# One table set for logarithm and exponential, reworked layer norms, and the last norm made in halves

## What is computed

```python
def _layer_norm(x, g, b):
    mu = jnp.mean(xf, axis=-1, keepdims=True)
    var = jnp.mean(jnp.square(xf - mu), axis=-1, keepdims=True)
    y = (xf - mu) * lax.rsqrt(var + LN_EPS)
    return (y * g + b)

def rmsnorm(x, g):
    y = x32 * lax.rsqrt(jnp.mean(x32 * x32, axis=-1, keepdims=True) + EPS)
    return (y * g)

# first block, per layer (0: attention, 1: retention)
h = _layer_norm(DEEPNORM_ALPHA * h + mix, ln_g[layer, 0], ln_b[layer, 0])
h = _layer_norm(DEEPNORM_ALPHA * h + _sq_relu_mlp(h, ffn_w1[layer], ffn_w2[layer]), ln_g[layer, 1], ln_b[layer, 1])
# second block
h = rmsnorm(x, norm_mix[layer])          # attention and state-space scan from h, added to x
h = rmsnorm(x, norm_ffn[layer])
x = x + (jax.nn.silu(gate) * val) @ w_ffn_down[layer]
return rmsnorm(x, norm_final)
```

## Time and profile before

| | us |
|---|---|
| median of 3 runs | 2658.95 (2658.17 to 2660.28) |
| span of the profiled execution, first to last instruction | 2656.4 |
| TensorE matmuls busy in it | 2615.0 |
| VectorE busy | 1675.5 |
| ScalarE busy | 1268.0 |

### The profile page before, as it was taken

How to read it: one execution, slowest core, us unless ns; L and a number is a source line. 1 busy time by engine, 2 the same in 40 slices (tenths; PEclk the granted TensorE clock), 3 DMA queues, 4 the chain that set the end, 5 groups by cost and what they waited for, 6 DMA issues and landing times.

```text
span 2656.4 us, 42476 instructions
## 1 busy us (share of the span) xinstructions
PE 2615.0 (98%) x16497; PEld 2236.1 (84%) x16497; DVE 1675.5 (63%) x2902; ACT 1268.0 (48%) x2049; POOL 183.4 (7%) x234
## 2 busy tenths in 40 slices
PE   9999999999999999999999999999999999999998
PEld 9877799999999798779898786766877777799996
DVE  4544586264565465487265535875589987696784
ACT  4556365153454354365154434254365564475561
POOL 1111000000000000100000012051000000000000
PEclk9999999999999999999999999999999999999999
DMA  9994936858556564736557979922433333254451
GB/s 355 222 230 119 216 92 234 207 165 248 135 171 212 146 184 140 232 110 196 145 164 245 260 187 266 253 66 80 145 94 114 119 111 120 81 189 148 156 174 56
DMA packets 187722, 450.56 MB, mean 170 GB/s; under 512 B 14984, under 2 KB 31368, under 8 KB 186896
## 3 DMA queue, kind: packets, MB, share of 16 engines
q1 hardware_dynamic: 108368, 264.29, 29.4%
q0 software_dynamic: 60000, 167.78, 26.7%
q10 hardware_dynamic: 19168, 15.93, 2.0%
HBM read 438.24 MB, written 159.51 MB: 225 GB/s over the span
## 4 chain that ended last, share of the span: by engine, by line
PE 85%; DVE 8%; ACT 4%; issue 2%; DMA 0%; POOL 0%; DVEq 0%; ACTq 0%; POOLq 0%
PE ps L399 29%; PE ps L1546 25%; PE ps L549 6%; PE ps L3344 4%; PE ps L2354 2%; PE ps L1991 2%; PE ps L2145 2%; PE ps L2029 2%; PE ps L2891 2%; PE ps L791 2%; PE ps L919 2%; DVE w_lo L370 1%; PE ps L878 1%; ACT w_hi L362 1%; DVE xs L3044 1%
## 5 line engine op out<-in xcount | busy, mean ns | idle before, releaser
L370 DVE TENSOR_TENSOR w_lo<-raw,w_hi 128x1024 fp32r<-128x1024 f32 x500 | 611.1, 1223 | 467.1 <-ACT w_hi L362 466.1
L362 ACT ACTIVATE w_hi<-raw 128x1024 fp32r<-128x1024 f32 x500 | 527.1, 1055 | 512.9 <-PE ps L399 292.3
L1546 PE MATMUL ps<-x_hi,w_hi 128*128 128x264 f32 (+1 forms) x1120 | 317.4, 283 | 2.1 <-DVE rg L1925 0.7
L1546 PE MATMUL ps<-x_hi,w_lo 128*128 128x264 f32 (+1 forms) x1120 | 316.3, 282 | 0.0
L1546 PE MATMUL ps<-x_lo,w_hi 128*128 128x264 f32 (+1 forms) x1120 | 316.1, 282 | 0.0
L399 PE MATMUL ps<-x_hi,w_hi 128*128 128x512 f32 (+1 forms) x688 | 248.3, 378 | 4.4 <-DVE x_lo L1410 2.7
L399 PE MATMUL ps<-x_lo,w_hi 128*128 128x512 f32 (+1 forms) x688 | 244.3, 372 | 0.0
L399 PE MATMUL ps<-x_hi,w_lo 128*128 128x512 f32 (+1 forms) x688 | 243.2, 371 | 0.0
L1546 PEld LDWEIGHTS ps<-x_hi,w_hi 128*128 128x128 f32 x1120 | 210.8, 188 | 5.0 <-issue 2.2
L1546 PEld LDWEIGHTS ps<-x_hi,w_lo 128*128 128x128 f32 x1120 | 211.1, 188 | 0.0
L1546 PEld LDWEIGHTS ps<-x_lo,w_hi 128*128 128x128 f32 x1120 | 210.6, 188 | 0.4
(11 more groups left out here) (503 smaller groups left out, 5827.8 us busy)
## 6 DMA issues: line engine op xcount, KB each, us to landing
raw<-in_weights SPq DMA_DIRECT2D x255, 512.0 KB
raw<-weight_sums SPq DMA_DIRECT2D x280, 256.0 KB
weight_sums<-in_weights POOLq DMA_DIRECT2D x36, 1536.0 KB, 19.4
raw<-in_weights SPq DMA_DIRECT2D x210, 256.0 KB
weight_sums<-in_weights POOLq DMA_DIRECT2D x12, 2048.0 KB, 31.1
weight_sums<-in_weights POOLq DMA_DIRECT2D x12, 1792.0 KB, 22.1
weight_sums<-weight_sums POOLq DMA_DIRECT2D x12, 1536.0 KB, 14.3
weight_sums<-weight_sums POOLq DMA_DIRECT2D x4, 2048.0 KB, 19.7
```

The costliest lines, as they stand in the source:

```text
L362: nc.scalar.activation(w_hi[:, s], raw[:, s], ACT.Copy).then_inc(hi_ready, 1)
L370: nc.vector.tensor_tensor(w_lo[:, s], raw[:, s], w_hi[:, s], ALU.subtract).then_inc(lo_ready, 1)
L1546: last = nc.tensor.matmul(out_, w[:, s, 4 * (b % 2) + k], a, start=kind in "125" and k == n == 0, stop=k == 3 and n == 2, skip_group_check ...
```

## The change

1. **One table set.** `load_exponents` loads a named set that holds both the logarithm and the exponential, once, and again only after a Silu or Sigmoid (`gate_function`). `load_logarithm` goes, with its one-column logarithm.
2. **Layer norms.** VectorE's multiplication by the root takes the gain g as well. ScalarE makes `x_hi` directly as xc + b; y follows two tiles behind, and `x_lo` is made from xc, b and `x_hi`. Four tiles instead of five are centred before the root, and the variance comes between the second and third. Where the norm is not wide (`ln10`, `ln11`), GpSimd centres tiles 5, 6 and 7 from the mean in SBUF, and VectorE reads the mean from PSUM, which lies a bank further. (A third call, in `ln01`, has an empty list of tiles, as the norm is wide.)
3. **RMS norms.** The low part is made one tile behind instead of two.
4. **Fewer placeholders.** Ahead of the sums 8 calls instead of 18 (`ln00`), none instead of 12 (`ln10`); behind them 18 instead of 27 (wide) and 17 instead of 26; 16 instead of 22 in RMS norms.
5. **The end in halves.** The last four output tiles of `fd2` are made for columns 0 to 255 first, then for 256 to 511, from the same weight chunks. The first half is normed and stored while the second is multiplied. `LastNorm` replaces `Norm` for `final`. Half 0 is stored in two pieces of four tiles, half 1 in four pieces of two.
6. The semaphore `zeroed` becomes `pool_made`, which counts GpSimd's centrings too.

```diff
-        def load_logarithm():
-            nc.scalar.activation(small[:, 14:15], small[:, 13:14], ACT.Ln)
+        def load_exponents():
+            if not table["exponents"]:
+                nc.scalar.preload_act_table_set("natural_log_exp_and_others")
+                table["exponents"] = True
+        def gate_function(out, in_, func):
+            table["exponents"] = False
+            return nc.scalar.activation(out, in_, func)
...
-                    idle_products(pe, 22)
+                    idle_products(pe, 16)
...
-                for k in range(KT + 2):
+                for k in range(KT + 1):
...
-                    if k >= 2 and not self.last:
-                        j = k - 2
+                    if k >= 1 and not self.last:
+                        j = k - 1
...
+                self.mean_at = 2048 if wide else 2560
+                self.by_pool = () if wide else (5, 6, 7)
...
+            def pool(self, pool):
+                c = slice(self.c0, T)
+                pool.wait_ge(ln_copied, 3 * self.nl + 2)
+                for k in self.by_pool:
+                    pool.wait_ge(ln_less, KT * self.nl + k + 1)
+                    nc.gpsimd.tensor_tensor(self.xc[:, k, c], self.xc[:, k, c], self.mean[:, c], ALU.subtract).then_inc(pool_made, 1)
...
-                idle_products(pe, {0: 18, 2: 12}.get(self.nl, 0), 6)
+                idle_products(pe, 8 if self.nl == 0 else 0, 6)
...
-                idle_products(pe, 27 if self.wide else 26)
+                idle_products(pe, 18 if self.wide else 17)
...
-            LESS_FIRST, Y_ON_ACT = 5, 2
+            LESS_FIRST, Y_ON_ACT, Y_BEHIND = 4, 2, 2
...
                 def less_mean(k):
+                    mean = self.mean[:, c] if self.wide else flat[:, self.mean_at:self.mean_at + SEQ]
...
-                    if k == 1:
+                    if k == 2:
...
+                later = {n: k for n, k in {1: 4, 2: 5, 3: 6, 5: 7}.items() if k not in self.by_pool}
...
-                        nc.vector.tensor_tensor(o, o, self.rt[:, c], ALU.mult).then_inc(norm_scaled, 1)
-                        if k in (1, 2, 4):
-                            less_mean({1: 5, 2: 6, 4: 7}[k])
+                        nc.vector.scalar_tensor_tensor(o, o, par[:, self.g + k:self.g + k + 1], self.rt[:, c],
+                                                       ALU.mult, ALU.mult).then_inc(norm_scaled, 1)
...
-                        nc.vector.tensor_tensor(x_lo[:, j, c], x32[:, j, c], x_hi[:, j, c], ALU.subtract).then_inc(norm_lo, 1)
+                        nc.vector.scalar_tensor_tensor(x_lo[:, j, c], self.xc[:, j, c], par[:, self.b + j:self.b + j + 1], x_hi[:, j, c],
+                                                       ALU.add, ALU.subtract).then_inc(norm_lo, 1)
+                    if k in later:
+                        less_mean(later[k])
...
+                        nc.scalar.activation(x_hi[:, k, c], self.xc[:, k, c], ACT.Identity, bias=b).then_inc(norm_hi, 1)
+                        if k >= self.Y_BEHIND:
+                            made(k - self.Y_BEHIND)
...
+        class LastNorm:
+            WHOLE, W = 4, SEQ // 2
...
+            def pe(self, pe):
+                for q in range(8):
+                    h, t, c = self.at_half(q)
...
+                    for r in range(8):
+                        for m, (w, a) in enumerate(((w_hi, ffn.f_hi), (w_hi, ffn.f_lo), (w_lo, ffn.f_hi))):
+                            last = nc.tensor.matmul(self.out(q), w[:, g % RING, r], a[:, r, c], start=r == 0 and m == 0, stop=r == 7 and m == 2)
+                    last.then_inc(chunk_done, 1)
+                    if q == 4:
+                        pe.wait_ge(sum_added, self.sums + 8)
+                        nc.tensor.matmul(self.mean(0), ones_d[:], x_sum[:, self.columns(0)], start=True, stop=True).then_inc(norm_var, 1)
+                pe.wait_ge(sum_added, self.sums + 11)
+                nc.tensor.matmul(self.mean(1), ones_d[:], x_sum[:, self.columns(1)], start=True, stop=False, skip_group_check=True)
+                idle_products(pe, 3, 4)
+                pe.wait_ge(norm_squared, self.squares_before + 1)
+                nc.tensor.matmul(self.mean(1), ones_d[:], self.sq[:], start=False, stop=True, skip_group_check=True).then_inc(norm_var, 1)
...
+            def dve(self, dve):
+                for q in range(8):
+                    self.half_tile(dve, q)
+                    if q == 4:
+                        dve.wait_ge(norm_root, self.n + 1)
+                    for k in {4: range(0, 2), 5: range(2, 5), 6: range(5, 8)}.get(q, ()):
+                        self.scale(0, k)
...
+            def store(self, sp):
+                before = KT * self.n
+                for k in range(0, KT, 4):
+                    sp.wait_ge(norm_scaled, before + k + 4)
+                    sp.dma_start(out[:, k:k + 4, 0:self.W], self.y[:, k:k + 4, 0:self.W]).then_inc(stored, 16)
+                for k in range(0, KT, 2):
+                    sp.wait_ge(norm_scaled, before + KT + k + 2)
+                    sp.dma_start(out[:, k:k + 2, self.W:SEQ], self.y[:, k:k + 2, self.W:SEQ]).then_inc(stored, 16)
```

More of the change, by code:

```diff
@@ L1152, in only_split @@
             side_stage(eng, split, name, None)
-        norms = {"all": 0, "layer": 0, "split": 0, "sums": 0, "squares": 0}
+        norms = {"all": 0, "layer": 0, "split": 0, "sums": 0, "squares": 0, "pool": 0, "centred": 0}
         sum_added = sem("sum_added")
@@ L3372, in pe @@
                         self.mixed_pe(pe, c)
-                for t in range(KT):
+                for t in range(LastNorm.WHOLE):
                     u = FIRST_TILE["fd2"] + t
@@ L3516, in program, with __init__, at_half, out @@
         rms_ffn = Norm("rms_ffn", FIRST_TILE["gv0"], PARAM["norm_ffn"], summed=True, xc_start=ffn.xc_start)
[L3518 removed]
+        class LastNorm:
+            WHOLE, W = 4, SEQ // 2
+            BANKS = (1, 3, 4, 5, 0, 2, 1, 3)
+            def __init__(self, g, start):
+                self.g, self.n = g, norms["all"]
+                self.sums, self.squares_before = norms["sums"], norms["squares"]
+                placed["next"] = start
+                self.y = at("final_y", [P, KT, SEQ])
+                self.sq = at("final_sq", [P, self.W])
+                self.rt = at("final_rt", [P, SEQ])
+                self.tile, self.chunk = FIRST_TILE["fd2"] + self.WHOLE, FIRST_CHUNK["fd2"] + self.WHOLE
+            def at_half(self, q):
+                return q // 4, self.WHOLE + q % 4, slice(self.W * (q // 4), self.W * (q // 4 + 1))
+            def out(self, q):
+                return ps[:, self.BANKS[q], 0:self.W]
+            def mean(self, h):
+                return ps[:, 6 + h, 0:self.W]
+            def columns(self, h):
+                return slice(META + self.W * h, META + self.W * (h + 1))
+            def pe(self, pe):
+                for q in range(8):
+                    h, t, c = self.at_half(q)
+                    if q >= 4:
+                        u = self.tile + q - 6
+                        pe.wait_ge(evicted[u % 2], u // 2 + 1)
+                    g = FIRST_CHUNK["fd2"] + t
+                    pe.wait_ge(lo_ready, g + 1)
+                    for r in range(8):
[10 more added lines that the diff above has]
+                nc.tensor.matmul(self.mean(1), ones_d[:], self.sq[:], start=False, stop=True, skip_group_check=True).then_inc(norm_var, 1)
+            def half_tile(self, dve, q):
+                h, t, _ = self.at_half(q)
+                u, half = self.tile + q, slice(self.W * h, self.W * (h + 1))
+                x, total = x32[:, t, self.columns(h)], x_sum[:, self.columns(h)]
+                dve.wait_ge(chunk_done, self.chunk + q + 1)
+                nc.vector.tensor_tensor(x, x, self.out(q), ALU.add).then_inc(evicted[u % 2], 1)
+                if q == 7:
+                    return
+                dve.wait_ge(evicted[u % 2], u // 2 + 1)
+                dve.wait_ge(sum_added, self.sums + 4 + q)
+                dve_chain.mark(nc.vector.tensor_tensor(x_square[:, half], x, x, ALU.mult))
+                dve_chain.settle(dve)
+                nc.vector.tensor_tensor(total, total, x_square[:, half], ALU.add).then_inc(sum_added, 1)
+            def scale(self, h, k):
+                half, c = slice(self.W * h, self.W * (h + 1)), self.columns(h)
+                nc.vector.scalar_tensor_tensor(self.y[:, k, half], x32[:, k, c], par[:, self.g + k:self.g + k + 1], self.rt[:, half],
+                                               ALU.mult, ALU.mult).then_inc(norm_scaled, 1)
+            def dve(self, dve):
[5 more added lines that the diff above has]
+                        self.scale(0, k)
+                dve.wait_ge(evicted[(self.tile + 7) % 2], (self.tile + 7) // 2 + 1)
+                dve.wait_ge(norm_root, self.n + 2)
+                for k in range(KT):
+                    self.scale(1, k)
+            def root(self, act, h):
+                half = slice(self.W * h, self.W * (h + 1))
```

(17 more changed lines are left out.)

110 lines of the change are left out of this document (68 added, 42 removed).

## The result

| | before | changed |
|---|---|---|
| median of the comparison, us | 2658.56 (4 runs, 2658.1 to 2660.28) | 2640.08 (4 runs, 2638.9 to 2642.57) |
| ratio | | 0.9929 (0.9915 to 0.9943) |
| span of the profiled execution | 2656.4 | 2639.3 |
| ScalarE's table loads | 60 | 31 |

18.5 us less, 0.4 from the forecast; the span is 17.1 shorter where 18.4 were forecast. The total hides errors of both signs, which the positions of TensorE's products in the two traces lay open.

A forecast was written before the change was run, and what follows sets the result against it. TensorE, busy 2615.0 of 2656.4 us, bounds the kernel, so only its waits and placeholders can be won. Gains 1.65 + 0.5 + 4.0 + 3.9 + 2.05 + 5.0 + 1.3 = 18.4 give span 2638.0, median 2640.5; range 2636 to 2647.

The forecast's parts named there:

- Table set: One set for logarithm and exponential takes a 1.28 us load off the chain wherever the root is awaited; attention gains 1.3.
- the loads in retention and state-space stages I count at nothing: Removed loads there gain 0, since weight products keep TensorE busy; 1.3 us each in favour if one or two covers fail.
- The drain of which the Trainium skill speaks: 1380 ns on top of each 1283 ns table load, making each removed load worth 2.66 us; the forecast did not count it.
- ln00, ln01, ln10: Layer norms: net gains 1.65, 0.5 and 4.0 us from earlier first products, less time given back where VectorE sets the pace.
- ln11 with rms_mix: Norm row: squares ending 2.05 us sooner, table 1.28, low part after two scales 0.6; gain 3.9 us, from 2.8 to 4.5.
- rms_ffn: RMS norm at 2293.61: helper logarithm 0.2, table 1.28, third scale 0.6; gain 2.05 us, from 1.5 to 2.1.
- third scale 0.6: In rms_ffn, the low part coming after two scales instead of three brings the first product 0.6 us sooner.
- The end: Last four tiles in halves, no table load left (two before), 49 ns a store packet assumed: net 5.0 us; 2.9 at 82 ns.
- Contention: Rival at two norms: GpSimd and VectorE hinder each other, 8.2 us lost, 2648.7 us; chance 0.08.
- 6 us of slack behind GpSimd: The forecast's argument against GpSimd and VectorE hindering each other in the two norms where GpSimd centres tiles.
- costs what it costs from SBUF: At ln10, VectorE reading the mean from PSUM takes as long as from SBUF, 0.69 us for the PSUM read.
- clock rival: Fewer placeholders idle TensorE; 1.2 GHz for eight steps after five gaps adds 57 us, 2697 us; chance 0.04.

The follow-up runs named there:

- experiment 1: Changed kernel with the first table load put back ahead of the wait for the first activations: span 2637.5 us against the changed kernel's 2639.3.
- e5: Kernel before with only the common table set added, without the helper logarithms: 2651.97 us, ratio 0.997, span 2647.9.
- e2: Changed kernel with GpSimd centring no tiles, so VectorE centres all in ln10 and ln11: span 2639.1 us.
- e4: Changed kernel with the low part made two tiles behind again in the RMS norms: span 2640.5 us.
- e11: Changed kernel with the first table load ahead of the wait and the low part two tiles behind in rms_ffn alone: 2638.88 us, ratio 0.9923, span 2636.1.
- e3: Changed kernel with GpSimd centring tiles 5 to 7 in the wide norms ln00 and ln01 too, VectorE reading the mean from SBUF there: span 2641.1 us.
- e6: Changed kernel with separate table sets, each logarithm and exponential having its load, helper logarithm ahead of the wait: 2655.82 us, ratio 0.9983, span 2654.8.
- e7: Changed kernel with the last norm and last four tiles whole as before, the table set kept: 2646.06 us, ratio 0.9948, span 2641.2.
- e10: Changed kernel with VectorE reading the mean from SBUF instead of PSUM in ln10 and ln11: 2648.57 us, span 2646.7.
- e12: The changed kernel run again unaltered, five executions: 2641.01 us, ratio 0.9927, span 2640.8.
- e8: Changed kernel with the numbers of placeholders of the kernel before: 2646.62 us, ratio 0.9948, span 2645.4.
- e13: e11 with GpSimd centring four tiles (4 to 7) instead of three in ln10 and ln11: 2641.14 us, ratio 0.9929, span 2638.3.

## Why the forecast held, and where not

**Table set.** Right at the norms and in attention (1.3 forecast, 1.4 found). Two steps of it failed. One is "the loads in retention and state-space stages I count at nothing, since TensorE is covered there by weight products": 2.55 us came from there (2.35 with what the sparse attention lost), because the cover holds on average and not at each hand-over; the 0.86 us wait for `c_row` stood in the trace of before. The forecast named this risk and its price, 1.3 us each in its favour, but put no term on it. The other: the load's new place at the start was not costed at all, 1.3 us (experiment 1). The drain of which the Trainium skill speaks (ScalarE: Activation LUTs, What ACT_TABLE_LOAD costs) is not seen here either: the activation follows the load of 6.28 at 7.58, 0.02 us behind its end. With the loads gone in e5, attention gained 1.4 us and the end 1.2, about one load's own 1.28 each and not 2.66.

**ln00, ln01, ln10.** Right in mechanism and size: first products 3.5, 1.9 and 3.8 us nearer (3.55, 1.9, 4.0), and 1.4 and 1.3 given back in ln00 and ln01 in steps that VectorE sets at 1.98 us (2.0). ln00 kept 0.45 more than forecast: the waits in its steps are of 0.18 to 0.28 us, those of ln01 of 0.33 to 0.35, not 0.5.

**ln11 with rms_mix.** Mis-sized by 0.65, of which 0.5 are missing by the end of the row of squares. The scales are held up by GpSimd's last 0.46 us (1.67 for the pair instead of 1.41), and the row of sixteen squares follows them; this explains 0.26 us, by which the first square comes sooner in e2. The rest is open.

**rms_ffn.** Right at the first product (2.0 for 2.05), wrong behind it. The term "third scale 0.6" moves TensorE's start, not the work of ScalarE and VectorE on which `f_u` depends: 0.85 is given back there. Then the drop costs 1.5, of which 1.4 return, since TensorE's next two waits, 0.85 and 0.57 us longer in e4 and e11, shrink by as much. One tile behind costs 0.3 in rms_ffn and is worth 0.55 in rms_mix.

**The end.** Right: 5.0. The packet's 46 ns were the unseen price. Its split was not: the halves give 3.7 us and the tables 1.3.

**Contention.** Right for the wrong reason. "6 us of slack behind GpSimd" is not what saves ln10: with the mean in SBUF the slack is the same and VectorE's pair takes 3.44 us. What saves it is that VectorE's second operand comes from PSUM, which the forecast costed at nothing ("costs what it costs from SBUF"). The edit is worth 4.2 us by the first products of the two norms and 6.5 with the drops that come without it. Without it, GpSimd's help of 1.6 us would have been a net loss. The Trainium skill's sentence (GPSIMD Engine Reference, Key points) that VectorE instructions with two SBUF inputs contend with GpSimd agrees with the pairs shown: 1.27 with one SBUF input, 3.44 and 3.53 with two. Who came first counts too: VectorE's weight split of ln10, with two SBUF inputs, was running when GpSimd's first tile began (1155.55), kept its 1.22 us, and GpSimd's tile took 1.60 instead of 1.27.

**Clock.** The forecast's clock rival had TensorE at 1.2 GHz for eight steps after each of five gaps, 57 us in all. That is not what came: drops of 3.4 us did, in some executions only. The fourteen profiles split by the wait for `f_u`: with 2.23 to 2.27 us (the changed kernel, e1, e2, e3, e6, e7, e10, e12) six of eight show a drop behind it; with 0.96 to 1.41 us (before, e4, e5, e8, e11, e13) none of six. So the drop goes with the longer wait, though not strictly. At 150 us seven of fourteen have one. The code up to there differs only in the place of the first load: six of the nine profiles with the late load dropped and one of the five with the early one, too few to say whether the change has a part in its -1.5. That the kernel before would show a drop in other executions is likely (it scattered from 2658.1 to 2664.46 over the comparisons) but no profile of it shows one. A third place is the change's own: in e3, e4 and e12 the clock fell at 10.7 to 11.7 us, behind waits of 1.9 to 2.1 us for the first product, and cost 1.5; with the early load that wait is 0.6 us at most and none of the five profiles drops there.

In sum: -1.3 (start), -1.5 (clock at 150), -0.95 (rms_ffn), -0.65 (ln11) against +2.35 (retention and state-space), +0.45 (ln00) and +0.3 (ln01, ln10, attention) give 17.1 - 18.4 = -1.3; the rest of the closeness is that the median lay 0.8 above the profiled span instead of 2.55. The mechanisms of the large terms were right; that the total came within 0.4 us is luck.

## What to carry to other kernels

When GpSimd takes over elementwise work, look at where the operands of VectorE's instructions beside it lie: moving one of them to PSUM was worth more (4.2 us) than GpSimd's help itself (1.6). A chain on ScalarE and VectorE made shorter pays in full only if the placeholders that fill TensorE's time are cut with it (ln00 in e5: 0.4 us instead of 1.3), and little where the next wait depends on that chain's end rather than its start. A table load that stood ahead of a wait can sink below it when it becomes an explicit call: look at the first one in the trace.

## What the hardware showed unexpectedly

- A VectorE instruction with two SBUF operands nearly stands still until the GpSimd instruction beside it is over, and ends 0.54 to 0.57 us behind it (e3, e10, e13 and the changed kernel): a pair takes 3.44 us instead of 1.27. GpSimd itself slows from 4.07 to 4.95 us for three tiles.
- TensorE's granted clock fell to 1.2 GHz for stretches of 3.4 us (twice 6.8, at 148 in e8 and e10, and once 10.2, in e6), after waits of TensorE of 1.75 to 3.3 us (near 150, of 0.84), in some executions and not in others, at a cost of 1.0 to 1.5 us for 3.4 us (4.7 for the long one).
- A drop ahead of a wait costs little: at 2310 us, 1.4 of the 1.5 us lost came back in the two waits behind it.
